# One-hot columns by VectorE per expert, half a weight tile in another place, and the first up products ahead of ten keys

## The reference, cut to what matters

```
comb   = grp_p * softmax(top_l)                       # two weights a token
expert = grp_idx * 8 + top_i                          # two experts a token
y      = (silu(xb @ w1[e]) * (xb @ w3[e])) @ w2[e]     # 1024 -> 512 -> 1024
out    = sum over the token's two experts of y * comb
```

## Time and profile before

| what | us |
|---|---|
| median of 3 runs | 1618.83 |
| profiled execution | 1615.83 |
| its span | 1614.0 |
| TensorE busy | 1319.3 (82%) |
| VectorE busy | 457.7 (28%) |
| ScalarE busy | 284.1 (18%) |
| GpSimd busy | 132.4 (8%) |
| hardware queue of the weights | 502.84 MB, 76.7% of 16 engines |
| chain that ended last | TensorE 52%, DMA 42%, VectorE 2% |

### The profile page before, as it was taken

The page is one execution under the profiler, slowest core; times in us unless marked ns, Lnnn a source line. Parts: engine busy times, 40 slices in busy tenths (PEclk is TensorE's granted clock), DMA queues, the critical chain, the costliest instruction groups (busy, mean ns, idle before and its releaser), DMA issues.

```text
span 1614.0 us, 27193 instructions
## 1 busy us (share of the span) xinstructions
PE 1319.3 (82%) x11722; PEld 745.9 (46%) x11722; DVE 457.7 (28%) x968; ACT 284.1 (18%) x634; POOL 132.4 (8%) x289
## 2 busy tenths in 40 slices
PE   5999999999999887787778689988886657666665
PEld 4765887888563332232223278677432212211211
DVE  1346337431463322222222243753510000000001
ACT  0101214650021110111011113332211101101001
POOL 4000013000000000000000004122000000000000
PEclk9999999999999989988999889998998787888878
DMA  9799665133479999999999691310899999999997
GB/s 346 280 389 340 189 235 178 65 108 133 158 277 421 428 427 428 429 428 428 428 428 426 289 339 54 97 56 3 358 426 427 427 428 428 428 428 429 428 427 295
DMA packets 86630, 513.98 MB, mean 318 GB/s; under 512 B 8537, under 2 KB 13066, under 8 KB 61842
## 3 DMA queue, kind: packets, MB, share of 16 engines
q1 hardware_dynamic: 82450, 502.84, 76.7%
q0 software_dynamic: 3424, 9.27, 1.6%
q10 hardware_dynamic: 672, 0.65, 0.1%
HBM read 507.84 MB, written 3.15 MB: 317 GB/s over the span
## 4 chain that ended last, share of the span: by engine, by line
PE 52%; DMA 42%; DVE 2%; issue 1%; ACT 1%; SPq 1%; POOL 0%; DVEq 0%; ACTq 0%
PE ps L1518 42%; DMA arena<-in_w_e_down 19%; DMA ring<-in_exp_w 19%; PE ps L2317 4%; DMA ring<-in_w_e_up 2%; PE ps L1610 2%; DMA ring<-in_w_in 1%; PE ps L2089 1%; PE ps L2567 0%; PE ps L1766 0%; SPq L653 0%; PE ps L1762 0%; PE ps L1565 0%; PE ps L2330 0%; PE ps L2118 0%
## 5 line engine op out<-in xcount | busy, mean ns | idle before, releaser
L1518 PE MATMUL ps<-ring,arena 128*32 128x512 f32 (+4 forms) x1844 | 268.1, 650 | 101.1 <-DMA ring<-in_exp_w 85.3
L1518 PE MATMUL ps<-ring,hTs 128*32 128x512 f32 (+2 forms) x992 | 214.7, 633 | 46.1 <-DMA ring<-in_w_e_up 25.0
L1518 PE MATMUL ps<-hTs,ring 128*128 128x256 f32 (+1 forms) x992 | 215.5, 381 | 0.0
L1518 PEld LDWEIGHTS ps<-ring,arena 128*32 128x32 f32 (+1 forms) x1844 | 81.8, 128 | 267.5 <-issue 178.9
L1518 PEld LDWEIGHTS ps<-hTs,ring 128*128 128x128 f32 (+1 forms) x992 | 182.9, 188 | 29.1 <-issue 4.5
L1518 PE MATMUL ps<-arena,vv 128*32 128x512 f32 (+2 forms) x560 | 92.1, 710 | 84.5 <-DMA arena<-in_w_e_down 78.0
L1518 PEld LDWEIGHTS ps<-ring,hTs 128*32 128x32 f32 (+1 forms) x992 | 76.1, 136 | 155.0 <-issue 106.4
L3142 DVE COPY hTs<-ps 64x512 f32<-64x512 f32 x32 | 22.2, 693 | 259.5 <-PE ps L1518 259.5
L1518 PE MATMUL ps<-arena,hTs 128*32 128x512 f32 x480 | 95.0, 632 | 0.0
L1518 PEld LDWEIGHTS ps<-arena,vv 128*32 128x32 f32 (+2 forms) x560 | 28.1, 142 | 132.4 <-DMA arena<-in_w_e_down 86.3
L1236 ACT COPY arena<-ps 128x512 f32<-128x512 f32 x32 | 18.7, 585 | 387.9 <-PE ps L2067 387.9
(11 more groups left out here) (473 smaller groups left out, 1470.9 us busy)
## 6 DMA issues: line engine op xcount, KB each, us to landing
ring<-in_exp_w SPq DMA_DIRECT2D x91, 2048.0 KB, 21.8
arena<-in_w_e_down SPq DMA_DIRECT2D x28, 2048.0 KB, 25.7
ring<-in_w_e_gate SPq DMA_DIRECT2D x24, 2048.0 KB, 32.1
ring<-in_w_e_up SPq DMA_DIRECT2D x24, 2048.0 KB, 37.7
ring<-in_w_in SPq DMA_DIRECT2D x22, 2048.0 KB, 13.7
ring<-in_ada_w SPq DMA_DIRECT2D x12, 2048.0 KB, 15.9
arena<-in_w_e_up SPq DMA_DIRECT2D x8, 2048.0 KB, 34.7
arena<-in_w_e_gate SPq DMA_DIRECT2D x8, 2048.0 KB, 33.2
```

The source lines that it names most:

```text
L1518: return nc.tensor.matmul(o, lhsT, rhs, start=start, stop=stop)
```

## The change

`onep1` is gone. `first1` holds the columns of the first four experts, in `arena(4)`. The columns of all experts are compared straight into `gatep1` and are there multiplied in place by the routing weights. The columns that `pick` needs from expert 4 on are made by VectorE, one expert at a time, at the end of its `picked`, from `rank1`; GpSimd's copies go. That leaves `arena(9)` free, and the first half of tile 7 is loaded there, ahead of the second half, both after the wait for `vm`; the wait for the keys goes from SyncE's order. The down product of expert 1 takes its first two row blocks from there. On TensorE the keys 6 to 15 move behind the branch: 6 to 9 behind pick(1), 10 to 15 behind place(1). `settled` leaves out the bank of the keys, and a wait for it stands behind up(1). ScalarE copies the keys out behind silu(0). The branch for all experts has the ten keys and the copy at its beginning.

```diff
-        onep1, gatep1 = v3(arena(9), TT), v3(arena(5), TT)
+        first1, gatep1 = v3(arena(4)[:, 1792:2048], TT), v3(arena(5), TT)
...
+        seventh = v3(arena(9), 2)
+        def down_rows(at, f):
+            return seventh[:, f, :] if at == 7 and f < 2 else tile_at1(at, (4, 1024))[:, f, :]
...
                 is_full(sp, J("vm"))
-                sp.dma_start(dst[:, 2:4, :], src[:, 2:4, :]).then_inc(arrive, 16)
-                tile_read(sp, N1 + ring1(7) - RING)
-                sp.dma_start(dst[:, 0:2, :], src[:, 0:2, :]).then_inc(arrive, 16)
+                sp.dma_start(seventh, src[:, 0:2, :]).then_inc(arrive, 16)
+                sp.dma_start(tile_at1(7, (4, 1024))[:, 2:4, :], src[:, 2:4, :]).then_inc(arrive, 16)
...
-                if ahead:
-                    n = CAP1 * (at + 2)
-                    nxt = bass.ds(turn * CAP1 + n, CAP1) if late else slice(n, n + CAP1)
-                    nc.gpsimd.tensor_copy(onehot1[:, at % 2], onep1[:, :, nxt]).then_inc(S("onehot1_ready"), 1)
...
             picked(0, 0)
-            is_full(act, J("km"))
-            frees(nc.scalar.copy(kmT, v3(bank(J("km")), 2)), J("km"))
+            def memory_keys():
+                is_full(act, J("km"))
+                frees(nc.scalar.copy(kmT, v3(bank(J("km")), 2)), J("km"))
...
                 silu1(0, 0)
+                memory_keys()
+                turned_out(0, 0)
                 for b in range(BANKS):
                     act.sem_inc(free[b], general_jobs[b])
-                turned_out(0, 0)
...
             place_rows(0, 0)
-            memory_keys(6, 16)
             fits = is_compact(pe)
...
                 up_compact(0, 0, 0)
                 pick(0, 1)
-                settled()
+                memory_keys(6, 10)
+                settled(b for b in range(BANKS) if b != J("km") % BANKS)
                 place_rows(0, 1)
+                memory_keys(10, 16)
                 pe.wait_ge(S("xe1_ready"), 2)
                 up_compact(0, 1, 2)
+                is_out(pe, J("km"))
...
-                ins = tt(v3(onep1[:, t, 0:P], 4), last(rank1[:, t, 0:4], CAP1), mid(C("ekey"), 4), ALU.is_equal)
+                ins = tt(v3(first1[:, t, :], 4), last(rank1[:, t, 0:4], CAP1), mid(C("ekey"), 4), ALU.is_equal)
...
-                tt(v3(onep1[:, t, P:], NE1 - 4), last(rank1[:, t, 4:], CAP1), mid(C("ekey"), NE1 - 4), ALU.is_equal)
+                tt(v3(gatep1[:, t, :], NE1), last(rank1[:, t, :], CAP1), mid(C("ekey"), NE1), ALU.is_equal)
...
                 tt(xe, xe, last(modc2[:, 0:8], CAP1), ALU.add).then_inc(S("xe1_ready"), 1)
+                late = not isinstance(turn, int)
+                if late or 2 <= at < NE1 - 2:
+                    nxt = bass.ds(turn + (at + 2), 1) if late else slice(at + 2, at + 3)
+                    tt(onehot1[:, at % 2], rank1[:, :, nxt].to_broadcast([P, TT, CAP1]), mid(C("ekey"), TT),
+                       ALU.is_equal).then_inc(S("onehot1_ready"), 1)
...
-                    ins = tt(v3(gatep1[:, t, :], NE1), v3(onep1[:, t, :], NE1), last(comb[:, t, :], CAP1), ALU.mult)
+                    ins = tt(v3(gatep1[:, t, :], NE1), v3(gatep1[:, t, :], NE1), last(comb[:, t, :], CAP1), ALU.mult)
```

More of the change, by code:

```diff
@@ L659, in halves_of_seventh @@
                 src, arrive = pxk(A["exp_w2"][e]), loaded[(N1 + ring1(7)) % RING]
-                dst = tile_at1(7, (4, 1024))
                 is_full(sp, J("vm"))
-                sp.dma_start(dst[:, 2:4, :], src[:, 2:4, :]).then_inc(arrive, 16)
-                tile_read(sp, N1 + ring1(7) - RING)
-                sp.dma_start(dst[:, 0:2, :], src[:, 0:2, :]).then_inc(arrive, 16)
+                sp.dma_start(seventh, src[:, 0:2, :]).then_inc(arrive, 16)
+                sp.dma_start(tile_at1(7, (4, 1024))[:, 2:4, :], src[:, 2:4, :]).then_inc(arrive, 16)
             def given_back(at, i=None):
@@ L891, in norm_rows, with gather1 @@
                 load(lnr2[:, 1, :], A["ln2_b"][0].partition_broadcast(P), "ln2_loaded")
-            def gather1(turn, at, ahead=True):
+            def gather1(turn, at):
                 late = not isinstance(turn, int)
@@ L909, in _ @@
                 pool.wait_ge(S("spread_ready"), 3)
-                gather1(0, 0, False)
-                gather1(0, 1, False)
+                gather1(0, 0)
+                gather1(0, 1)
                 gather1(0, 2)
@@ L918, in _ @@
                 norm_rows()
-                gather1(0, NE1 - 2, False)
-                gather1(0, NE1 - 1, False)
+                gather1(0, NE1 - 2)
+                gather1(0, NE1 - 1)
             pool.wait_ge(S("down_done"), NE1)
@@ L1978, in pick @@
                         q = 2 * half + t
-                        one = onehot1[:, at % 2, t, :] if buffered else onep1[:, t, CAP1 * at:CAP1 * at + CAP1]
+                        one = onehot1[:, at % 2, t, :] if buffered else first1[:, t, CAP1 * at:CAP1 * at + CAP1]
                         ins = mm(ps[32 * q:32 * q + 32, 1536:2048], one, h2[:, t, 512 * half:512 * half + 512])
@@ L1998, in _, with settled @@
             place_rows(0, 0)
-            memory_keys(6, 16)
             fits = is_compact(pe)
-            def settled():
-                for b in range(BANKS):
+            def settled(banks=range(BANKS)):
+                for b in banks:
                     is_out(pe, max(q for q in range(J("general")) if q % BANKS == b))
@@ L2029, in down @@
             def down(turn, at, pos):
-                wt = tile_at1(pos, (4, 1024))
                 arrived1(turn, pos)
                 for f in range(4):
+                    wt = down_rows(pos, f)
                     pe.wait_ge(S("hid_ready"), turn * 4 + (4 * at + f + 1))
@@ L2039, in down @@
                                                    hid[:, f, t * P:(t + 1) * P],
-                                                   wt[:, f, half * 512:half * 512 + 512], start=False, stop=True,
+                                                   wt[:, half * 512:half * 512 + 512], start=False, stop=True,
                                                    skip_group_check=True)
@@ L2079, in down_compact @@
                             ins = mm(ps[32 * q:32 * q + 32, 1024:1536], HT1[:, 32 * f:32 * f + 32],
-                                     wt[:, f, half * 512:half * 512 + 512], i == 0, i == 1)
+                                     down_rows(pos, f)[:, half * 512:half * 512 + 512], i == 0, i == 1)
                 ins.then_inc(S("down1_full"), 1)
@@ L2158, in _ @@
             with pe.If(fits < 1):
+                memory_keys(6, 16)
                 pe.wait_ge(S("xe1_ready"), 1)
```

## The result

The changed kernel takes 1621.24 us, the median of 20 runs (1618.36 to 1626.54), against 1618.76 for the kernel before (20 runs, 1612.64 to 1620.40): a ratio of 1.0022, with a 95% interval of 1.0014 to 1.0030. By the ratio it is slower by about 3.5 us; the two medians lie 2.5 us apart. The forecast was 0.4 us faster.

A forecast was written before the change was run, and what follows sets the result against it. Weight landings were taken to set the mixture's pace, so the gain was idle time removed from the weight queue: 0.1 with full clock loss, 1.8 with none, 0.4 taken, giving 1618.4 us, range 1614.8 to 1621.5.

The forecast's parts named there:

- so a shift of the stream goes through to the end one for one: Behind the first mixture everything starts from its last product, so time gained in the weight stream shortens the whole kernel equally.
- The sum: Steps from up(0) to weight 12's start in the first mixture: gain 0.1 to 0.7 us with clock loss, 0.4 taken.
- Rival B: TensorE's flag read and branch show ahead of up(0): slower than before, up to 1.0 us, 1619.8; chance 0.12.
- 3.10 was reckoned: TensorE's up(0) waits for picked(0,0) behind place(0) and 2.02 us of idle, and starts at 472.32.
- a hole of 2.42 us: Nearest priced hole in TensorE's own issue, used as the branch's price: up(0) 0.4 us later and the gain gone.
- +0.30 us on the spread: VectorE's two spread operations grow from 896 to 1024 elements, 2.09 to 2.39 us, ahead of picked(0,0).
- the one-hot: 28 VectorE operations of 0.23 us replace GpSimd copies, hidden under 4.51 us of VectorE idle: cost nothing; uncovered, 6.4 us.
- up(1) at 3.64 with no idle ahead: On TensorE, moved keys cover both old idles ahead of up(1), which then takes 3.64 us at clock 1.00.
- the 1.1 to 1.7: Loss in us from TensorE's low clock on up(0), which lies between 3.64 and 5.34; middle 1.4.
- the gain of 0.1 to 0.7 us: Earlier start of weight 12: 0.1 us with the whole clock loss, 0.7 with a loss of 1.1.
- rival A: TensorE's clock stays up around up(0): 1.8 us faster, 1617.0; chance 0.20.
- rival D: Later waits of the weight queue, such as weight 12's for the combine, take all gain back: 1618.8; chance 0.12.

The follow-up runs named there:

- e5: Changed kernel with 217 more instructions in TensorE's never-run branch, its second-block code 256 further on than in the kernel before: 1618.64 us, ratio 1.0008.
- e1: Kernel before with 39 instructions (waits) added in TensorE's never-run branch: 1623.31 us, ratio 1.0027.
- e2: Changed kernel without the ten keys in TensorE's never-run branch and with one more wait there, code position as before: 1618.55 us, ratio 0.9999.
- e11: e2 with 17 instead of 1 in the never-run branch, TensorE's second-block code 16 instructions further on than before: 1618.58 us, ratio 0.9994.
- e7: Kernel before with 64 instructions added in TensorE's never-run branch: 1627.41 us, ratio 1.0056.
- e10: e2 with 225 instead of 1 in the never-run branch, TensorE's second-block code 224 instructions further on than before: 1618.02 us, ratio 1.0000.
- e12: e2 with 241 instead of 1 in the never-run branch, TensorE's second-block code 240 instructions further on than before: 1619.71 us, ratio 1.0005.
- e3: Kernel before with only VectorE's part: one-hot columns per expert, all columns straight into the gates, GpSimd's copies gone: 1617.63 us, ratio 0.9988.
- e4: Kernel before with the changes of e3 and the seventh weight's two halves issued side by side: 1618.02 us, ratio 0.9993.
- e6: Kernel before with 128 instructions added in TensorE's never-run branch: 1622.23 us, ratio 1.0020.
- e8: Kernel before with 192 instructions added in TensorE's never-run branch: 1619.74 us, ratio 1.0007.
- e9: e2 with SyncE's old order: second half of the seventh weight, wait for the keys, then first half: 1624.94 us, ratio 1.0038.

## Why the prediction was wrong, and where it was right

**Wrong: the step "so a shift of the stream goes through to the end one for one", and with it the keys' second copy, which has no term in the sum.** The sum ended with the mixture, and it had no term for the keys' second copy: the part by part reckoning priced instructions that run and none that is only passed over. 39 more of these moved TensorE's code against the period of 256 instructions at which its holes stand (e5), and that costs 1.0027 by itself (e1), while the changed kernel without them is at 0.9999 (e2) and with 217 more at 1.0008 (e5). The interval of e1 holds the whole 1.0022, and those of e2 and e5 hold 1 (those of e2 and e11 also end below that of the changed kernel, at 1.0011 and 1.0005; that of e5 reaches 1.0021). Rival B had the right kind of stall, one of TensorE's own issue, in the wrong place: at the branch it never showed (up(0) starts 3.08 us after place(0) in the profile after, 3.10 was reckoned), while some 570 us later it did. The earlier trace rows was the hint: a hole of 2.42 us of "issue" in straight-line code was read as a price for a branch, and not asked about for itself.

In the stretch of the scans, whose products are as short as 32 columns, the holes are a visible part of the time: 8.2 (e11) to 15.0 us (e7) of them from 1015 to 1160 us, by position.

**Right: the mixture.** +0.30 us on the spread was +0.27, the one-hot 0.22 for 0.23, up(0) starts as reckoned, up(1) at 3.64 with no idle ahead. With the low clock on up(0) (e2, e5, e10: 0.50 over 3 us, 4.95 to 4.97 for the product, a loss of 1.3, inside the 1.1 to 1.7) weight 12 goes out 28.2 us after place(0), where the old order has 28.1 to 28.4 (26.7 in e7), and the mixture takes 460.2 to 460.8 against 460.0 to 461.5. These ranges lie over each other: the gain of 0.1 to 0.7 us that the forecast rests on is neither shown nor refuted. With the clock up (changed, e12: 1.00 from 470 to 492 us) weight 12 goes out after 26.9, and the mixture takes 459.0 twice: rival A's 1.8 us lies within the 1.0 to 2.5 that this is below the old order. Both occur in the new order, and a third case does that had no rival: 6.59 us for up(0), over the 5.34 that the prediction took as the most, and 463.1 for the mixture (e11), slower than the old order. In the old order the low level, where it comes, falls on up(1) (0.50 from 482.5 to 485.75 before, over 3.3 us in e1, e3, e4, e6 and e8, not at all in e7), and it costs little: with up(1) at 3.64 (e7) the mixture is 460.4, with 5.06 to 5.12 it is 460.0 to 460.8, with 5.33 and 5.34 it is 460.8 and 461.5. So the issue of weight 12 is no measure of the gain: in e7 it comes as early as in the changed kernel and brings nothing. What the mixture follows is the rate of the queue in the 100 us from place(0) on: 394 to 397 GB/s in the old order, 395 to 396 in the new with 4.95 to 4.97 for up(0), 401 with the clock up, 389 in e11 and 363 in e9. The change moved the clock's low stretch from a product that the queue doesn't wait for to one that it does.

**Left open.** The two profiles differ by 5.2 us from the rank to the end, more than the medians. 3.2 of it are the scans and -2.5 the mixture; 2.1 lie in the second mixture (418.6 us between its first and last product of 64 columns from line 2625, against 416.5; 416.2 to 417.7 in the twelve runs), 1.4 in the last 16 us and the rest between the stretches. In the last stretch the granted clock of the profile after was 0.83 against 0.94. That mean doesn't explain it, since e1 and e2 have 14.5 us there, like the kernel before, at 0.84 and 0.86, and e5 has 15.9 at 0.84. It may be a matter of the products on which the low level falls; that was not tried.

No version beats the kernel before clearly. The best ratio is e3's 0.9988; the whole change at a good position (e2, e10, e11) is at 0.9994 to 1.0000, with intervals within 0.9983 to 1.0014. That holds the forecast and rival D, by which the gain doesn't reach the end, alike.

## What to carry to other kernels

A change's size is also its instructions that never run: if the program behind them has stretches of short instructions with "issue" holes, compare the two programs' lengths first, and test by padding a branch that isn't run, once with the same number and once with as many as fill up the period of the holes (256 here, e5). And before idle time is moved in front of the product that a queue waits for, ask where the clock's low stretch lay before; where it lay, it may have been free (here the mixture took 460.0 us with 5.12 us for up(1), e6, and 460.4 with 3.64, e7).

## What the runs showed of the hardware

- In the stretch of the scans, whose products are as short as 32 columns, TensorE's own issue has holes: 88 of 0.5 us and more in fourteen profiles between 1040 and 1112 us, up to 2.65 us (e1), once 4.83 (e7). Their period is 256 instructions: the first three have 18, 36 and 104 records of their groups left at position 0 and again at 256 (e5), 37, 55 and 123 at 39. Position alone moved the whole kernel by up to 1.0056 (e7).
- The instruction queue moves packets of 16.4 KB (66 of them, 1.08 MB, in the profile after), and 86 of the 88 holes end 1.2 to 1.6 us after one has landed.
- Such a packet went out 4.3 us after the stretch of 256 instructions before it was entered, and not 1.1 to 1.8 as elsewhere ahead of the first scan's third hole, when 2 MB of weights were moving (e7).
- The first scan's loop, 397 instructions and so longer than the period, had two holes inside its first turn at position 128 (e6) and none inside the three later ones, which began 0.29 to 0.44 us after the turn before had ended; one instruction packet went out in their 8.9 us.
- The granted clock is 1.00 or 0.50 in the fourteen profiles. The same 32 products of up(0), behind the same 2.0 us of idle, took 3.64 (twice), 4.95 to 4.97 (three times), 5.21 and 6.59 us in seven profiles, by how much of them ran at 0.50: none in the profile after, the part from 474.58 to 477.2 in e2, from 474.12 to 480.1 in e11.
